# Attention steps in a fixed order, a later conv norm, an output projection over eight banks, and two of four conv tiles moved to ScalarE and GpSimd

## The reference

```python
def even_mixer(h, w_in, b_f, conv_w, conv_b, conv_norm, q_norm, k_norm, w_out):
    z = h @ w_in                                  # h is rmsnorm(x)
    u, g, q, k, v, f_logit = jnp.split(z, splits, axis=-1)      # 512 each, f_logit 8
    a = u * jax.nn.sigmoid(g)
    a = causal_depthwise_conv(a, conv_w) + conv_b               # 31 taps
    a = jax.nn.silu(rmsnorm(a, conv_norm))
    q = rmsnorm(q.reshape(b, s_len, 8, 64), q_norm)
    k = rmsnorm(k.reshape(b, s_len, 8, 64), k_norm)
    v = v.reshape(b, s_len, 8, 64)
    log_f = jax.nn.log_sigmoid(f_logit + b_f)
    o = forgetting_attention(q, k, v, log_f)      # blocks of 128 queries, causal
    return jnp.concatenate([a, o], axis=-1) @ w_out
```

## Time and profile before

| | us |
|---|---|
| median of 3 runs | 1962.81 (1962.69 to 1965.41) |
| the profiled execution, its own time | 1965.04 |
| its span, first to last instruction | 1963.2 |
| TensorE busy | 1889.5 (96% of the span) |
| VectorE busy | 915.5 (47%) |
| ScalarE busy | 621.6 (32%) |
| GpSimd busy | 330.2 (17%) |
| mean granted TensorE clock | 0.979 |
| chain that ended last | TensorE 88%, VectorE 7%, ScalarE 2%, issue 2%, GpSimd 1% |

### The profile page before, as it was taken

The page is one execution under the profiler, slowest core; times in us unless marked ns, Lnnn a source line. Parts: engine busy times, 40 slices in busy tenths (PEclk is TensorE's granted clock), DMA queues, the critical chain, the costliest instruction groups (busy, mean ns, idle before and its releaser), DMA issues.

```text
span 1963.2 us, 22410 instructions
## 1 busy us (share of the span) xinstructions
PE 1889.5 (96%) x8333; PEld 1540.9 (78%) x8333; DVE 915.5 (47%) x1016; ACT 621.6 (32%) x803; POOL 330.2 (17%) x276
## 2 busy tenths in 40 slices
PE   7999999998876899999999999999999999999999
PEld 5888888875555688888888888888888888888887
DVE  6443433379875564343334443433365454343321
ACT  4333332225433443333223333332222333333221
POOL 3111101115444211111101111110113021111000
PEclk9999999999877899999999999999999999999999
DMA  5333333221100143333332333343233333333431
GB/s 142 99 98 96 102 111 100 75 79 54 32 1 6 56 121 96 96 96 108 103 99 75 96 96 96 96 118 99 72 97 96 97 97 96 96 96 100 118 105 42
DMA packets 341356, 174.86 MB, mean 89 GB/s; under 512 B 6256, under 2 KB 340284, under 8 KB 341308
## 3 DMA queue, kind: packets, MB, share of 16 engines
q1 hardware_dynamic: 337052, 172.12, 30.3%
q10 hardware_dynamic: 4256, 2.11, 0.4%
HBM read 172.10 MB, written 2.10 MB: 89 GB/s over the span
## 4 chain that ended last, share of the span: by engine, by line
PE 88%; DVE 7%; ACT 2%; issue 2%; POOL 1%; DMA 0%; SPq 0%; ACTq 0%; POOLq 0%; DVEq 0%
PE bank L1188 29%; PE bank L1189 29%; PE bank L1190 29%; DVE conv L901 3%; DVE w_lo L871 1%; DVE pt_lo L1094 1%; ACT w_hi L587 0%; DMA x_rows<-in_x 0%; DVE h_rough L1032 0%; PE bank L1417 0%; POOL probs_a L547 0%; POOL conv L559 0%; PE bank L1244 0%; DVE neg_max L1087 0%; ACT probs_a L737 0%
## 5 line engine op out<-in xcount | busy, mean ns | idle before, releaser
L871 DVE TENSOR_TENSOR w_lo<-raw,w_hi 128x1024 fp32r<-128x1024 f32 (+2 forms) x308 | 403.0, 1309 | 718.6 <-ACT w_hi L587 718.2
L1188 PE MATMUL bank<-xg_hi,w_hi 128*128 128x512 f32 x1728 | 678.3, 393 | 8.1 <-DVE w_lo L871 4.8
L1189 PE MATMUL bank<-xg_lo,w_hi 128*128 128x512 f32 x1728 | 674.0, 390 | 0.0
L1190 PE MATMUL bank<-xg_hi,w_lo 128*128 128x512 f32 x1728 | 673.8, 390 | 0.0
L587 ACT ACTIVATE w_hi<-raw 128x1024 fp32r<-128x1024 f32 (+2 forms) x308 | 340.3, 1105 | 793.0 <-PE bank L1190 792.9
L1188 PEld LDWEIGHTS bank<-xg_hi,w_hi 128*128 128x128 f32 x1728 | 325.4, 188 | 86.3 <-issue 10.8
L1189 PEld LDWEIGHTS bank<-xg_lo,w_hi 128*128 128x128 f32 x1728 | 325.5, 188 | 68.1 <-issue 1.2
L1190 PEld LDWEIGHTS bank<-xg_hi,w_lo 128*128 128x128 f32 x1728 | 325.3, 188 | 67.8
L1188 PE MATMUL bank<-h_hi,w_hi 128*128 128x512 f32 x704 | 274.5, 390 | 0.0
L1190 PE MATMUL bank<-h_hi,w_lo 128*128 128x512 f32 x704 | 274.0, 389 | 0.0
L1189 PE MATMUL bank<-h_lo,w_hi 128*128 128x512 f32 x704 | 273.9, 389 | 0.0
(11 more groups left out here) (184 smaller groups left out, 1171.3 us busy)
## 6 DMA issues: line engine op xcount, KB each, us to landing
raw<-in_ffn_w_gate SPq DMA_DIRECT2D x88, 512.0 KB, 3.8
raw<-in_ffn_w_up SPq DMA_DIRECT2D x88, 512.0 KB, 3.8
raw<-in_ffn_w_down SPq DMA_DIRECT2D x64, 704.0 KB, 4.5
raw<-in_od_w_in SPq DMA_DIRECT2D x24, 512.0 KB, 3.7
raw<-in_ev_w_in SPq DMA_DIRECT2D x20, 512.0 KB, 3.8
raw<-in_ev_w_out SPq DMA_DIRECT2D x16, 256.0 KB, 2.7
raw<-in_od_w_out SPq DMA_DIRECT2D x8, 512.0 KB, 3.7
x_rows<-in_x SPq DMA_DIRECT2D x4, 512.0 KB, 7.4
```

The source lines that it names most:

```text
L871: dve.tensor_tensor(w_lo[:, u % 2, 0:n], raw[:, u % 4, 0:n], raws(w_hi[:, u % 2, 0:n]), ALU.subtract)\
L1188: pe.matmul(dst, a[0], b[0], start=start, stop=False)
L1189: pe.matmul(dst, a[0], b[1], start=False, stop=False)
L1190: return pe.matmul(dst, a[1], b[0], start=False, stop=stop)
```

## The change

It changes orders and shares of work; what is computed stays.

- **Attention steps.** `every` and fixed offsets replace the lags: in step t VectorE takes `row_inv` of pair t - 1, `neg_max` of pair t, then `cat_lo`, then `pt_lo` of pair t - 3, then one tap (`TAPS_T` = 1). ScalarE takes `cat_hi`, `pt_hi` of pair t - 3, then the exponentials of pair t. GpSimd scales pair t - 1. TensorE turns pair t - 2; weighing begins at step 5 (par 0) and 6 (par 1). There are 22 steps.
- **Three fans** (5, 6, 7) with their `qk_low` and `qk_high` move from the v phase to steps 0, 1, 2, into banks 6 and 7. `head_sum` comes one unit later, with four buffers for the squares. `head_fan` is built in two halves.
- **v** is made hi tile by tile as its bank is done (`v_done`).
- **Conv.** VectorE has tiles 0 and 2, ScalarE and GpSimd 1 and 3. ScalarE's taps now stand in the gated units (13), the q and k units (29), the v phase (12, between the `qk_high` calls) and steps 0 to 3 (8). L901 reads `a_in` in SBUF as before.
- **Conv norm.** Squares in steps 4, 6, 8 and 14, the sum at step 16 in bank 3, the root at 17, reciprocals at 18 and 19, `a_rstd` at 20. silu and splitting of the conv tiles move into the first units of the output projection (`SILU_AT`).
- **Output projection.** `out_unit` takes the attention half of all eight output tiles first (groups 0 and 1, eight banks), then the conv half. The first three k of units 0 and 1 are done in steps 18 and 19 (`merge_part`).

```diff
-    DVE_TILES, ACT_TILES = list(range(CB - 1)), [CB - 1]
-    TAPS_A, TAPS_QK = [7, 7, 8, 8], [2, 4, 4, 3, 4, 0, 4, 4]
-    TAPS_T = 3
-    ACT_TAPS_QK, ACT_TAPS_V = [0, 3, 4, 4, 4, 4, 4, 4], 4
+    DVE_TILES, ACT_TILES = [0, 2], [1, 3]
+    TAPS_A, TAPS_QK = [0, 4, 3, 4, 4, 4, 4, 4], [2, 2, 4, 2, 4, 1, 4, 4]
+    TAPS_T = 1
+    ACT_TAPS_A, ACT_TAPS_QK, ACT_TAPS_V, ACT_TAPS_T = [3, 3, 4, 3], [2, 3, 4, 4, 4, 4, 4, 4], [4, 4, 4], 2
...
-    V_FANS = [(1, 1), (1, 3), (2, 1), (2, 3), (3, 0), (3, 2)]
+    V_FANS = [(1, 2), (2, 1), (3, 1)]
...
+    INV_AT, TURN_AT, PT_AT, PV_AT, OUT_AT = 1, 2, 3, 5, 8
+    STEPS = TB * (AB - 1) + OUT_AT + 2
+    NEXT_SPLIT = (12, 14)
+    A_SQ, A_SUM = [4, 6, 8, 14], PAIRS
+    MERGE_AT = (STEPS - 4, STEPS - 3)
+    SILU_AT = [(0, 2), (0, 3), (1, 0), (1, 1)]
...
         def out_unit(g, u):
-            return g // 2 * 4 + u, (1 - g % 2) * CB
+            return g % 2 * 4 + u, CB if g < 2 else 0
...
@@ GpSimd, the steps @@
                     for t in range(STEPS):
-                        if t < PAIRS:
-                            for i in (2 * t, 2 * t + 1):
+                        if 0 <= t - INV_AT < PAIRS:
+                            pool.wait_ge(inv_ready, t - INV_AT + 1)
+                            for i in (2 * (t - INV_AT), 2 * (t - INV_AT) + 1):
...
+                        if t < 4:
+                            add_taps(ACT_TAPS_T)
+                        if t in A_SQ[1:]:
...
@@ ScalarE, the v phase @@
                     qk_high(0)
                     split_hi(ph, 0, 2)
+                    conv_taps(ACT_TAPS_V[0])
                     qk_high(1)
+                    conv_taps(ACT_TAPS_V[1])
                     qk_high(2)
+                    split_hi(ph, 0, 3)
+                    conv_taps(ACT_TAPS_V[2])
                     qk_high(3)
-                    split_hi(ph, 0, 3)
-                    conv_taps(ACT_TAPS_V)
-                    for n in range(AB, QK - 1):
-                        qk_high(n)
-                    act.wait_ge(unit_done, ph.unit0 + ph.units)
+                    qk_high(4)
                     act.wait_ge(col_ready, 1)
                     for tb in range(TB):
+                        if tb < TB - 1:
+                            act.wait_ge(v_done, tb + 1)
+                        else:
+                            act.wait_ge(unit_done, ph.unit0 + ph.units)
...
@@ VectorE, the output projection @@
-                        if g % 2 == 1:
+                        if g >= 2:
...
                         split_lo(ph, g, u + 2)
+                        if (g, u) in SILU_AT:
+                            b = SILU_AT.index((g, u))
+                            dve.wait_ge(ahi_ready, b + 1)
+                            dve.tensor_tensor(cat_lo[:, b, :], a_act[b][:, :], raws(cat_hi[:, b, :]), ALU.subtract)\
+                                .then_inc(alo_ready, 1)
...
@@ TensorE, the steps @@
                 for t in range(STEPS):
-                    if t == A_SUM:
-                        pe.wait_ge(exp_done, 2 * t - 2)
...
                     if t < PAIRS:
                         scores(t)
+                    if t == A_SUM:
+                        pe.wait_ge(exp_done, 2 * t)
+                        pe.wait_ge(a_added, CB - 1)
+                        pe.matmul(bank[3][:, :], ones[:, :], sq_sum[:, :], start=True, stop=True).then_inc(a_sum, 1)
+                    if QK - 3 + t < QK:
+                        fan(QK - 3 + t)
+                    for par in range(2):
+                        chunk = every(t, PV_AT + par, 2, CHUNKS)
+                        if chunk is not None:
+                            weigh(chunk, par)
+                    if 0 <= t - TURN_AT < PAIRS:
+                        turn(t - TURN_AT)
+                    if t in MERGE_AT:
+                        n = MERGE_AT.index(t)
+                        pe.wait_ge(wlo_ready, A_OUT.unit0 + n + 1)
+                        merge_part(A_OUT, 0, n, list(range(CB - 1)))
```

More of the change, by code:

```diff
@@ L465, in add_taps, with build_fan @@
                 pool_taps[0] += n
+            def build_fan(n):
+                pool.memset(head_fan[n][:, :, :], 0.0).then_inc(fan_ready, 1)
+                pool.wait_ge(fan_ready, 3 * n + 1)
+                for half in range(2):
+                    view = head_fan[n][:, half::2, :].rearrange("r j (a c) -> r j a c", a=2)
+                    pool.affine_select(out=view, in_=view, compare_op=ALU.not_equal, fill=1.0,
+                                       base=-2 * (half * AB + n * AB // 2),
+                                       pattern=[[-2, AB // 2], [-1, 2], [0, HD]], channel_multiplier=1)\
+                        .then_inc(fan_ready, 1)
+                pool.wait_ge(fan_ready, 3 * n + 3)
             def gates(ph):
@@ L483, in gates @@
                 one(1, 1)
-                with pool.Fori(1, n // 2) as g:
-                    for par in range(2):
-                        one(g * 2 + par, par)
+                if ph is A_GATE:
+                    for f in range(2, n):
+                        one(f, f % 2)
+                        add_taps(ACT_TAPS_A[2 * f - 4])
+                        add_taps(ACT_TAPS_A[2 * f - 3])
+                else:
+                    with pool.Fori(1, n // 2) as g:
+                        for par in range(2):
+                            one(g * 2 + par, par)
             for ph in phases:
@@ L625, in group @@
                             act.activation(acted[:, par, :], gate[:, par, :], func).then_inc(gate_acted, 1)
+                        if ph is A_GATE and not first:
+                            conv_taps(ACT_TAPS_A[u])
                         if u % 2 == 1 and ph.gate == "silu":
@@ L1072, in attention @@
                 split_lo(ph, 0, 3)
-                for n in range(AB, QK - 1):
-                    qk_low(n)
+                qk_low(AB)
                 for tb in range(TB):
@@ L1310, in turn_out, with merge_part @@
                 last.then_inc(out_turned, 1)
+            def merge_part(ph, g, u, ks):
+                wh, wl = weights(ph, u)
+                tile, k0 = out_unit(g, u)
+                for k in ks:
+                    if g == 0 and u == 0:
+                        pe.wait_ge(olo_ready, 2 * k + 2)
+                    elif g == 2 and u == 0:
+                        pe.wait_ge(alo_ready, k + 1)
+                    last = product(bank[tile][:, :], (wh[:, k, :], wl[:, k, :]),
+                                   (cat_hi[:, k0 + k, :], cat_lo[:, k0 + k, :]), g < 2 and k == 0, g >= 2 and k == CB - 1)
+                if ks[-1] == CB - 1:
+                    last.then_inc(unit_done, 1)
             def merge(ph):
@@ L1315, in merge @@
                         pe.wait_ge(wlo_ready, 4 * g + ph.unit0 + u + 1)
-                        wh, wl = weights(ph, u)
-                        tile, k0 = out_unit(g, u)
-                        for k in range(CB):
-                            if g == 0 and u == 0:
-                                pe.wait_ge(olo_ready, 2 * k + 2)
-                            elif g == 1 and u == 0:
-                                pe.wait_ge(alo_ready, k + 1)
-                            last = product(bank[tile][:, :], (wh[:, k, :], wl[:, k, :]),
-                                           (cat_hi[:, k0 + k, :], cat_lo[:, k0 + k, :]),
-                                           g % 2 == 0 and k == 0, g % 2 == 1 and k == CB - 1)
-                        last.then_inc(unit_done, 1)
+                        merge_part(ph, g, u, [CB - 1] if g == 0 and u < 2 else list(range(CB)))
             def attention():
```

226 lines of the change are left out of this document (110 added, 116 removed).

## The result

The changed kernel takes 1934.45 us (median of 4 runs, 1933.3 to 1936.8); the kernel before takes 1964.11 on the same chips (1962.69 to 1965.47). The ratio is 0.9851, with a 95% interval of 0.9834 to 0.9868: 29.7 us saved, where 17.6 were forecast.

The account below looks back on a forecast made before the run. Attention, with TensorE at a 0.74 clock, was the largest reserve; VectorE set the pace in q and k. First scores +4.5, attention -12.6, output projection -9.5: -17.6 from 1962.8 gave 1945 us; own range 1938 to 1951, overall 1932 to 1957.

Parts of the forecast that it names:

- rival A: Products in the v stage covered, first scores at 541, TensorE warm, attention 88 us: 29 us saved, 1934; chance 0.19.
- q and k units: Before the v projection: VectorE loses taps but GpSimd's additions slow the rest; qk_raw(7) at about 500.5, 0.5 us saved.
- The bound "4 us saved": Favourable bound for gated projection, q and k units, if additions miss the taps.
- v projection: ScalarE's products between the norms delay the last w_lo; first scores 548.6 instead of 544.1, 4.5 us lost with the earlier part.
- Steps 0 to 5: First part of attention: GpSimd's 8 additions and scalings take 22.4 us, turning pair 3 waits for them; 29 us together.
- Steps 6 to 15: Middle of attention: no wait for pt_hi, one tap instead of three; 4.6 us per step instead of 5.65, 46 us.
- The loop: In steps 6 to 15, scores, neg_max, pt_lo and turn space the steps: 16.5 us per four, 18.2 at lowered clock.
- the bound of 84 "at full clock": Lower bound for the length of all attention, forecast at 92 us, if the loop ran at full clock.
- Tail: Steps 16 to 21: waits for last exponentials, reciprocals and last cat_lo, beside weighing and 18 output matmuls; 17 us.
- Output projection: Attention half over eight banks covers the conv norm, silu and cat_lo; 42 us instead of 51.5, 9.5 saved.
- B: Attention step stays long: TensorE's clock stays low, early steps wait longer for GpSimd; attention 100 us, 1953; chance 0.15.
- C: GpSimd's additions become the bound beside VectorE's work: nothing saved at 2.02 us per pair, 1969 at 2.15; chance 0.06.

Follow-up runs that it names:

- e5: Changed kernel with each of GpSimd's 60 additions of tap products on one column instead of about 500, sums of conv tiles 1 and 3 left out: 1911.76 us.
- e4: Changed kernel with ScalarE's twelve products of the v projection all behind k_hi(3) instead of between the q and k norms: 1931.15 us.
- e1: Changed kernel with ScalarE's order alone taken back, exponentials ahead of cat_hi and pt_hi in each attention step: 1953.99 us.
- e12: Kernel before with ScalarE's new order of attention steps alone; pt_hi, pt_lo and the weighing come one step later: 1955.58 us.
- e2: Changed kernel with the old order of the output projection, banks 0 to 3 finished first: 1938.78 us.
- e7: Kernel before with the eight-bank output projection alone, attention half of all eight tiles first: 1959.15 us.
- e3: Changed kernel with two VectorE taps per attention step instead of one, and twelve fewer in the q and k units: 1933.82 us.
- e9: Changed kernel with the old conv share: three tiles on VectorE with three taps per step, one tile on ScalarE with GpSimd: 1937.48 us.
- e11: Kernel before with the conv norm's sum behind all steps and the eight-bank output projection together: 1956.69 us.
- e10: Changed kernel with ScalarE's v products behind k_hi(3) and two VectorE taps per step from step 4, fewer beside q and k units: 1927.51 us.
- e13: e10 with three VectorE taps per step from step 4 instead of two, and eleven fewer beside the q and k units: 1922.55 us.

## Why the prediction was right, and where its terms were not

The direction and most mechanisms were right; that 1934 lies inside the stated range is owed to the share given to rival A, not to the forecast's own sum, whose range (1938 to 1951) the result misses. By its terms the forecast was +4.5 to the first scores, -12.6 in attention, -9.5 in the output projection, together -17.6. Measured, as lengths within the mixer stage, are +0.5, -22.7 and -8.0, together -30.2. Step by step:

- *q and k units.* Forecast 0.5 us saved, measured 3.4: qk_raw(7) came at 496.1, not at 499 to 502. The mis-sized term is the taps: I had 23 x (0.75 + 0.8 x 0.8) = 32 us, and they took 27.7, 1.20 us per tap, which is 0.57 of them slowed by 0.8. GpSimd was busy for 48.2 of 62 us, the 0.8 that I had, so its busy share isn't the share of taps that it slows. Nor was its share before the 68% that I gave: 35.0 of 65 us are 54%. That the taps met additions less often because VectorE's other work met them too fits the slower w_lo and corrections (e5), but was not counted. The bound "4 us saved" was near.
- *v projection.* Forecast 5 us lost from qk_raw(7) to the first scores, measured 3.9. The last w_lo ended 37.4 us after the start of qk_raw(7) (forecast 37 to 38, before 32.1), TensorE idled for 11.5 us where I had some 10, and the first scores came 9.5 us after w_lo, not 10.1:

```profile
496.09 0.68 DVE L1200 TENSOR_TENSOR qk_raw<-bank,rstd 128x512 f32<-128x512 f32 x1
...
532.24 1.22 DVE L903 TENSOR_TENSOR w_lo<-raw,w_hi 128x1024 fp32r<-128x1024 f32 x1
```

  The mechanism is the one foretold, shown by e4: taking the products away from between the norms gives 3.3 us of it back. First scores came at 542.98, 5.6 us ahead of the 548.6 forecast: 1.5 of it from the earlier start of the stage, 2.9 from the q and k units, 1.2 from here.
- *Steps 0 to 5.* Forecast 29 us, measured 28.4, in part by luck. GpSimd's additions and scalings of four pairs took 19.8 us, not 22.4, and by the profile TensorE waited for them only at pair 0 (2.6 us in two waits); pair 3 was turned without such a wait, and thin additions shorten steps 0 to 3 by 2.4 us (e5). Beside that it waited 3.5 us for pt_lo and ran at half its clock from 550.5 to 564.2 us, for which the sum had no term.
- *Steps 6 to 15.* Forecast 46, measured 40.2. This is the largest error. The loop was right (that it passes through pt_hi's place in ScalarE's order is shown by e1 and e12), and so was its sum of 16.5 us for four steps at full clock; measured are 16.2 and 16.8. What I added to it, 1.7 us for a clock of 0.8 to 0.85 and 0.3 for a step that exceeds the loop, did not come: TensorE was granted 0.96. Attention as a whole, 81.9 us, came out below even the bound of 84 "at full clock". I had taken the clock as a property of the stage, and it changes with the order alone (e1: 0.80 against 0.89 over the same four steps): in after TensorE is busy 34.3 of 40.2 us.
- *Tail.* Forecast 17, measured 13.3: the clock is 1.00 there, and a single long gap is left, 1.88 us for the last cat_lo. The wait for sq_sum is gone, as foretold.
- *Output projection.* Forecast 42 us, measured 43.6: the wait for the third w_lo was 1.3 us (forecast 1), and the low clock, 0.55 from 624.9 to 632.5, cost some 2.8 (43.6 - 39.5 - 1.3; forecast 1.5). Of the 8.0 us saved 4.1 are the 18 matmuls moved into the steps. The other 3.9 are the cause given, products for eight banks in front of the conv half: taking it back costs 3.7 here (e2), and e7 gains 4.0 by it.

Rival A had the time (1934) but not the way: it had the first scores earlier through products that were covered, which e4 shows they were not; its second half, that TensorE stays warm in attention, is what happened from step 6 on, and by more (81.9 us, not 88). B is refuted: steps 6 to 15 had a clock of 0.96, and the 0.70 of steps 0 to 5 didn't make them longer than forecast. Of C, the additions beside the taps, the mechanism is real and large: it costs 22.7 us in after (e5). It doesn't decide the sign, because a pair takes 1.6 us and not more. The Trainium skill ("SBUF — State Buffer", Who interferes with whom) says that a VectorE operation with two SBUF inputs contends with a GpSimd one that reads SBUF, and that one of the two holds the shared ports for its whole instruction while the other "fully blocks". The first half agrees with the rows: taps lose, and see below what doesn't. The second isn't borne out in full: alone 0.75 and 1.27 us, together 1.6 and not 2.02, also in e3 (3.23 for two).

What the parts are worth, one at a time, put into the kernel before: order of ScalarE -8.1, late sum +2.1, eight banks -4.0, late sum and eight banks together -7.0. All of the change but the moved tile (e9) gives -25.7. The parts don't add up: -8.1 and -7.0 leave 10.6 us missing. By the table nearly all of it stands behind the neg_max of step 12: tail and output projection together, where the moved matmuls don't matter, grow by 1.9 us in e12, shrink by 6.7 in e11 and by 15.1 in e9. The tail shows what they need of each other: the order of ScalarE lengthens it by 4.9 us in the kernel before (e12) and shortens it by 8.3 in after (e1 against after). The waits of e12 point to the squares in consecutive steps, which after has spread out. But this is read from one trace: no run puts the spread squares and the late sum alone beside the order, and e9 also has the fans, GpSimd's scaling one step later, the v stage's order and the step numbers of after.

## What to carry to other kernels

Where steps of a pipeline are spaced by a loop through several engines, find the operation in it that stands behind work needed less soon. Moving it ahead cost one step more of distance here, and it returned more than its wait, since TensorE's granted clock rose too (e1). Try an edit of this kind together with what is late next: the tail gave back 4.9 of the 9 us when it was tried alone (e12). Fill the slack of such a loop with work from stages where it hurts (e10, e13), but not beside GpSimd's additions of two tiles (e3). And when work moves from one stage into another, compare the two stages at equal work before a gain is put down to a cause.

## What the runs showed of the hardware

- Longer waits cost TensorE clock as well: with only ScalarE's order changed, 100 matmuls of four steps took 13.86 us at 0.89 and 16.20 at 0.80 (e1). Three parts of attention have 0.70, 0.96 and 1.00 with TensorE busy 78%, 85% and 85% of the time, so the busy share of a part alone doesn't tell its clock. Nor did the 0.70 follow directly on the idle wait of 11.5 us in the v stage: from 537 to 550.5 us TensorE was granted its full clock, and only then half of it, until 564.2 (after):

```profile
537.00:550.50 13.50, 12.62 (x61) 7.25 (x59) 8.88 (x14) 7.64 (x14) 3.32 (x10) 1.00 0.00 0
550.60:564.10 13.50, 9.02 (x39) 6.12 (x38) 9.14 (x18) 9.47 (x24) 13.21 (x12) 0.50 0.00 0
```

- What GpSimd's additions slow on VectorE, means over the stretch ahead of attention, after against e5: taps 1148 against 812 ns, w_lo (1024 columns) 1485 against 1292, h_corr 1338 against 676. What they don't slow: qk_raw, which reads PSUM and one tile of SBUF (673 against 676), and the reciprocal h_rough (3333 in both).
- Beside GpSimd's scalings of the probabilities, which read one tile and a column, taps lose little: in e10 two of them took 1.68 us while a pair of scalings of 384 columns ran throughout, and 2.39 us in the step in which GpSimd added up sq_sum.
